# Gathered expert features: high and low parts in one tile, interleaved word by word

## The chip, the cores and the metric

The kernel runs on one core of a Trainium2 chip. The metric is device time in microseconds (us) from start to end of one execution; the figure given is the median of several.

## What is computed

Two layers of a streaming encoder for 256 prompt tokens and 64 running tokens (320 in all, D_MODEL 1024), float32. Each layer mixes three head groups and then applies a feed-forward part; in the second layer this is a mixture of eight SwiGLU experts of width 3584, of which each token uses two:

```python
logits = jnp.dot(xt, w_r, preferred_element_type=F32)
top_v, top_i = lax.top_k(logits, TOP_K)
w = jax.nn.softmax(top_v, axis=-1)
gates = jnp.einsum('tk,tke->te', w, jax.nn.one_hot(top_i, N_EXPERTS, dtype=F32))
...
for e in range(N_EXPERTS):
    h = jax.nn.silu(xt @ wg[e]) * (xt @ wu[e])
    y = y + gates[:, e:e + 1] * jnp.dot(h, wd[e], preferred_element_type=F32)
```

## The kernel before

Every large product is made with numbers split in two: a high part in float32r (TensorE's reduced float32) and a low part that is what the rounding left. A product is three matmuls: high by high, low by high, high by low.

The dense part (layers 1 and 2 without the experts) takes weights in cuts of 1024 words a partition as the stationary operand and the 320 tokens as the moving one (`three`, L1986 and following; the helper's line is L1981).

The experts run after it, one after another. For each, up to 128 tokens are gathered by row into `xg`, transposed by TensorE in eight blocks of 128 (`xg_T`, L2419; the helper's line is L1984) into two PSUM banks, and split there: ACT scales and rounds each block to `xgT_hi` (`xg_hi`, L1249), DVE computes what is left into `xgT_lo` (`xg_lo`, L1817). Both are tiles of 128 partitions, 8 blocks (`KB`), 128 tokens. They are the stationary operands of gate and up; the expert's weights move, 512 columns at a time.

Weights come in pieces of 2048 words a partition (1 MB), 42 pieces (`NP`) an expert: 14 of gate and 14 of up, taken in turns, then 14 of down. SyncE issues one DMA a piece into `raw`, seven slots deep, each as soon as DVE has released the slot. ACT rounds the piece to `split_hi` (L1207), DVE computes `split_lo` (L1808), both three slots deep (`SR`). TensorE (`experts`, L2439) makes twelve matmuls of a piece: for gate and up, high weights by `xgT_hi` (L2475) and by `xgT_lo` (L2479), then low weights by `xgT_hi` (L2484); in the very first piece the ones by `xgT_lo` come last (L2489). After silu and product (`hm`), four transposes (L2528) turn each 512 columns of hidden values; they load `hm[:, m % 2, k:512:4]`, every fourth word, as their stationary operand, and ACT and DVE split the result into `hmT_hi` and `hmT_lo`, the stationary operands of down (L2510, L2513, L2519, and L2495, L2496, L2502 for the last piece).

At `X_AT`, the third piece from the end of an expert (`NP - 3`), ACT and DVE make the next expert's `xgT_hi` and `xgT_lo` between their pieces; TensorE transposes `xg` four pieces earlier. The order on every engine is the program's; the waits are semaphores.

The last expert's output isn't scattered by DMA but placed by matmuls (L2544 to L2552). Its high and low parts are `last_y_hi` and `last_y_lo`, which before lie in the memory of `xgT_hi` and `xgT_lo`, and are the moving operand there.

Of the kernel before, what the change touches and what calls it, by code (L numbers as in the profile page):

```python
# [17 lines left out]
FR = mybir.dt.float32r  # L18
# [7 lines left out]
P = 128  # L26
D = 1024
KB = D // P
# [220 lines left out]
def build(nc, A, O):  # L249
# [5 lines left out]
    with ExitStack() as ctx:  # L255
        def sb(name, shape, dt=F32, stack=ctx):
            return stack.enter_context(nc.sbuf_tensor(name, shape, dt))
# [197 lines left out]
        isc_s = sb("isc_s", [P, 1], U32)  # L455
        last_token = sb("last_token", [P, 48])[:, 0:1]
        xg = sb("xg", [P, D])
        xgT_hi = sb("xgT_hi", [P, KB, P], FR)
        xgT_lo = sb("xgT_lo", [P, KB, P], FR)
        hs = sb("hs", [P, 2, 512])  # L460
        first_only = ExitStack()
        Gown = sb("Gown", [P, NT, P], F32, first_only)
# [3 lines left out]
        loop_only = ExitStack()  # L466
        hmT_lo = sb("hmT_lo", [P, FEB, P], FR, loop_only)
        loop_only.close()

        def raw_piece(i):  # L470
            s = PSLOT[i % PR]
            return raw[:, s * PIECE:(s + 1) * PIECE]
# [90 lines left out]
            eng.wait_ge(cv_out, 16 * 2 * DEPTH)  # L563

        HALVES = [slice(0, 512), slice(512, 1024)]
        last_y_hi = xgT_hi[:].rearrange("p k n -> p (k n)")
        last_y_lo = xgT_lo[:].rearrange("p k n -> p (k n)")

        def y_rows_of(t, c):
            return y_p[0, P * t:P * t + P, c] if t < 2 else y_s[0, :, c]  # L570
# [2036 lines left out]
```

## Time and profile before

| | |
|---|---|
| time, median of 3 runs | 1535.76 us (1535.21 to 1536.22) |
| span of the profiled execution | 1535.8 us |
| PE busy | 1527.8 us (99%), 8428 matmuls |
| PEld busy (weight loads) | 1333.0 us (87%) |
| DVE busy | 1234.4 us (80%) |
| ACT busy | 998.9 us (65%) |
| POOL busy | 217.5 us (14%) |
| DMA | 437.43 MB, mean 285 GB/s |

The span goes from the first to the last instruction of the profiled execution, which has no time of its own beside it. PE is TensorE's matmuls, PEld its weight loads, which overlap them; matmuls are pipelined, and the recorded length of one reaches into the next, so the distance between starts is what paces the engine. L12 is line 12 of the kernel.

### The profile page before, as it was taken

The page shows a single profiled execution, that of the slowest core. Times are in us where ns is not written, and L with a number is a line of the kernel's source. Part 1 is how long each engine was busy: PE and PEld are TensorE (multiplying, and loading weights), DVE is VectorE, ACT ScalarE, POOL GpSimd, SP SyncE. Part 2 cuts the span into 40 slices and gives each one's busy share as a digit, 9 for nine tenths or more (in the row PEclk, how much of TensorE's full clock was granted, in tenths as well). Part 3 has the DMA queues.
Part 4 walks back from the last instruction along what each step waited for, and adds up shares of the span by engine and source line. Part 5 has one row for each costly group of instructions (what it writes and reads, how often), then busy time and mean ns, then how long its engine had stood idle before and what let it go on. Part 6 is the DMA issues. An engine that isn't in the chain of part 4 may idle for free.

```text
span 1535.8 us, 21611 instructions
## 1 busy us (share of the span) xinstructions
PE 1527.8 (99%) x8428; PEld 1333.0 (87%) x8428; DVE 1234.4 (80%) x1253; ACT 998.9 (65%) x1079; POOL 217.5 (14%) x249
## 2 busy tenths in 40 slices
PE   9999999999999999999999999999999999999998
PEld 7989999999998988888888888888888888888887
DVE  5877666654477758988988888998998988898897
ACT  5655433333466547777777778777777777777775
POOL 5514400001150403101001001002002002002000
PEclk9999999999999999999999999999999999999999
DMA  8333455444443459999999999999999999999994
GB/s 226 96 110 116 149 164 164 133 157 151 125 122 110 141 209 367 383 366 388 372 381 376 374 374 376 391 359 386 384 363 382 381 362 379 400 361 363 394 373 183
DMA packets 159701, 437.43 MB, mean 285 GB/s; under 512 B 12068, under 2 KB 66176, under 8 KB 145264
## 3 DMA queue, kind: packets, MB, share of 16 engines
q1 hardware_dynamic: 151796, 423.02, 75.0%
q0 software_dynamic: 5552, 9.62, 2.3%
q10 hardware_dynamic: 2252, 3.41, 0.7%
q8 instruction: 68, 1.11, 0.3%
q14 instruction: 33, 0.27, 0.1%
HBM read 429.40 MB, written 13.60 MB: 288 GB/s over the span
## 4 chain that ended last, share of the span: by engine, by line
PE 98%; DMA 0%; ACT 0%; DVE 0%; issue 0%; SPq 0%; DVEq 0%; ACTq 0%
PE bank L1981 34%; PE bank L2475 13%; PE bank L2484 13%; PE bank L2479 13%; PE bank L2510 6%; PE bank L2513 6%; PE bank L2519 6%; PE bank L1984 3%; PE bank L2528 2%; PE bank L2496 0%; PE bank L2502 0%; PE bank L2495 0%; DMA gla<-b_g 0%; DVE x L1972 0%; ACT L1076 0%
## 5 line engine op out<-in xcount | busy, mean ns | idle before, releaser
L1808 DVE TENSOR_TENSOR split_lo<-raw,split_hi 128x2048 fp32r<-128x2048 f32 x336 | 763.1, 2289 | 101.8 <-ACT split_hi L1207 100.8
L1207 ACT CAST split_hi<-raw 128x2048 fp32r<-128x2048 f32 x336 | 640.5, 1911 | 224.5 <-PE bank L2484 145.7
L2475 PE MATMUL bank<-split_hi,xgT_hi 128*128 128x512 f32 x896 | 291.7, 395 | 0.0
L2479 PE MATMUL bank<-split_hi,xgT_lo 128*128 128x512 f32 x892 | 285.8, 390 | 0.0
L2484 PE MATMUL bank<-split_lo,xgT_hi 128*128 128x512 f32 x896 | 239.9, 390 | 0.0
L913 ACT CAST cut_hi<-ring 128x1024 fp32r<-128x1024 f32 x124 | 129.9, 1048 | 166.6 <-PE bank L1981 166.6
L1981 PE MATMUL bank<-xT_hi,cut_hi 128*128 128x320 f32 x752 | 236.7, 315 | 0.0
L1981 PE MATMUL bank<-xT_hi,cut_lo 128*128 128x320 f32 x752 | 233.5, 310 | 0.0
L1981 PE MATMUL bank<-xT_lo,cut_hi 128*128 128x320 f32 x752 | 231.9, 308 | 0.0
L1346 DVE TENSOR_TENSOR cut_lo<-ring,cut_hi 128x1024 fp32r<-128x1024 f32 x124 | 153.0, 1235 | 80.7 <-ACT cut_hi L913 79.9
L2484 PEld LDWEIGHTS bank<-split_lo,xgT_hi 128*128 128x128 f32 x896 | 168.3, 188 | 34.9
L2479 PEld LDWEIGHTS bank<-split_hi,xgT_lo 128*128 128x128 f32 x892 | 167.7, 188 | 34.7
L2475 PEld LDWEIGHTS bank<-split_hi,xgT_hi 128*128 128x128 f32 x896 | 166.2, 189 | 32.3
L1981 PEld LDWEIGHTS bank<-xT_hi,cut_hi 128*128 128x128 f32 x752 | 142.1, 189 | 1.6
L1981 PEld LDWEIGHTS bank<-xT_lo,cut_hi 128*128 128x128 f32 x752 | 142.2, 189 | 0.0
L1981 PEld LDWEIGHTS bank<-xT_hi,cut_lo 128*128 128x128 f32 x752 | 142.0, 189 | 0.0
L2510 PE MATMUL bank<-split_hi,hmT_hi 128*128 128x512 f32 x416 | 129.8, 393 | 0.0
L2513 PE MATMUL bank<-split_hi,hmT_lo 128*128 128x512 f32 x416 | 128.3, 390 | 0.0
L2519 PE MATMUL bank<-split_lo,hmT_hi 128*128 128x512 f32 x416 | 111.3, 390 | 0.0
L853 POOL COPY idc<-idx 128x1 uint32 (+1 forms) x8 | 5.7, 707 | 635.9 <-PE bank L1984 616.0
L2513 PEld LDWEIGHTS bank<-split_hi,hmT_lo 128*128 128x128 f32 x416 | 78.2, 188 | 16.3
L2519 PEld LDWEIGHTS bank<-split_lo,hmT_hi 128*128 128x128 f32 x416 | 78.1, 188 | 16.2
(316 smaller groups left out, 1723.2 us busy)
## 6 DMA issues: line engine op xcount, KB each, us to landing
raw<-moe_w_gate SPq DMA_DIRECT2D x112, 1024.0 KB, 7.8
raw<-moe_w_up SPq DMA_DIRECT2D x112, 1024.0 KB, 7.6
raw<-moe_w_down SPq DMA_DIRECT2D x112, 1024.0 KB, 7.3
ring<-w_in SPq DMA_DIRECT2D x15, 1024.0 KB, 5.5
ring<-ffn_w_gate SPq DMA_DIRECT2D x11, 1024.0 KB, 5.5
ring<-ffn_w_up SPq DMA_DIRECT2D x11, 1024.0 KB, 5.4
ring<-ffn_w_down SPq DMA_DIRECT2D x10, 1024.0 KB, 5.1
ring<-w_out SPq DMA_DIRECT2D x8, 1024.0 KB, 5.0
```

Source lines behind the costliest of these rows:

```text
L913: nc.scalar.copy(split_cut(cut_hi, q), raw_cut(q)).then_inc(cut_hi_ready, 1)
L1207: return nc.scalar.copy(split_hi[:, i % SR, :], raw_piece(i)).then_inc(hi_ready, 1)
L1346: V.tensor_tensor(split_cut(cut_lo, q), raw_cut(q), split_cut(cut_hi, q).bitcast(F32), ALU.subtract).then_inc(cut_lo_ready, 1)
L1808: V.tensor_tensor(split_lo[:, i % SR, :], raw_piece(i), split_hi[:, i % SR, :].bitcast(F32), ALU.subtract).then_inc(lo_ready, 1)
L1981: return TE.matmul(out, lhsT, rhs, start=start, stop=stop)
L1984: return TE.transpose(out, in_, ident[0:rows, 0:rows])
L2475: TE.matmul(o, xgT_hi[:, kk, :], hi[:, w * k + 512 * c:w * k + 512 * c + 512], start=kk == 0, stop=False)
L2479: TE.matmul(o, xgT_lo[:, kk, :], hi[:, w * k + 512 * c:w * k + 512 * c + 512], start=False, stop=False)
L2484: last = TE.matmul(o, xgT_hi[:, kk, :], lo[:, w * k + 512 * c:w * k + 512 * c + 512], start=False, stop=kk == KB - 1)
L2510: TE.matmul(banks[6 + n][:], hmT_hi[:, b, :], hi[:, c], start=b == 0, stop=False)
L2513: TE.matmul(banks[6 + n][:], hmT_lo[:, b, :], hi[:, c], start=False, stop=False)
L2519: last = TE.matmul(banks[6 + n][:], hmT_hi[:, b, :], lo[:, c], start=False, stop=b == FEB - 1)
```

## The change

The two tiles become one with a last dimension of two: word 0 is the high part, word 1 the low part of the same token. `xgT_hi` and `xgT_lo` are views of it. So ACT's and DVE's writes, DVE's read of the high part, and the stationary operands at L2475, L2479, L2484 and L2489 step by two words. `last_y_hi` and `last_y_lo` get tiles of their own, placed on the stack over the memory of `hmT_lo`.

```diff
--- before.py
+++ after.py
@@ -455,8 +455,8 @@
         isc_s = sb("isc_s", [P, 1], U32)
         last_token = sb("last_token", [P, 48])[:, 0:1]
         xg = sb("xg", [P, D])
-        xgT_hi = sb("xgT_hi", [P, KB, P], FR)
-        xgT_lo = sb("xgT_lo", [P, KB, P], FR)
+        xgT = sb("xgT", [P, KB, P, 2], FR)
+        xgT_hi, xgT_lo = xgT[:, :, :, 0], xgT[:, :, :, 1]
         hs = sb("hs", [P, 2, 512])
         first_only = ExitStack()
         Gown = sb("Gown", [P, NT, P], F32, first_only)
@@ -466,6 +466,8 @@
         loop_only = ExitStack()
         hmT_lo = sb("hmT_lo", [P, FEB, P], FR, loop_only)
         loop_only.close()
+        last_y_hi = sb("last_y_hi", [P, D], FR)
+        last_y_lo = sb("last_y_lo", [P, D], FR)
 
         def raw_piece(i):
             s = PSLOT[i % PR]
@@ -563,8 +565,6 @@
             eng.wait_ge(cv_out, 16 * 2 * DEPTH)
 
         HALVES = [slice(0, 512), slice(512, 1024)]
-        last_y_hi = xgT_hi[:].rearrange("p k n -> p (k n)")
-        last_y_lo = xgT_lo[:].rearrange("p k n -> p (k n)")
 
         def y_rows_of(t, c):
             return y_p[0, P * t:P * t + P, c] if t < 2 else y_s[0, :, c]
```

## Rows read from the trace of the kernel before

**Rows 1.** The page: the span, and TensorE's granted clock in tenths, 40 slices.
```profile
span 1535.8 us, 21611 instructions
...
PEclk9999999999999999999999999999999999999999
```

**Rows 2.** Busy us (x instructions) of PE, PEld, DVE, ACT, POOL; clock, DMA share, GB/s.
```profile
0.00:560.00 560.00, 557.00 (x3986) 528.24 (x3987) 371.78 (x654) 267.80 (x522) 133.28 (x172) 0.99 0.45 140
...
576.50:1527.00 950.50, 950.47 (x4325) 791.73 (x4325) 845.25 (x549) 719.45 (x541) 81.75 (x74) 1.00 0.98 371
```

**Rows 3.** The chain of work that ended last, shares of the span by line.
```profile
PE bank L1981 34%; PE bank L2475 13%; PE bank L2484 13%; PE bank L2479 13%; PE bank L2510 6%; PE bank L2513 6%; PE bank L2519 6%; PE bank L1984 3%; PE bank L2528 2%; PE bank L2496 0%; PE bank L2502 0%; PE bank L2495 0%; DMA gla<-b_g 0%; DVE x L1972 0%; ACT L1076 0%
```

**Rows 4.** Groups by line and form: count, busy us, mean ns, idle before.
```profile
L2475 PE MATMUL bank<-split_hi,xgT_hi 128*128 128x512 f32 x896 | 291.7, 395 | 0.0
L2479 PE MATMUL bank<-split_hi,xgT_lo 128*128 128x512 f32 x892 | 285.8, 390 | 0.0
L2484 PE MATMUL bank<-split_lo,xgT_hi 128*128 128x512 f32 x896 | 239.9, 390 | 0.0
...
L2475 PEld LDWEIGHTS bank<-split_hi,xgT_hi 128*128 128x128 f32 x896 | 166.2, 189 | 32.3
...
L2528 PEld LDWEIGHTS bank<-const_sb,hm 128*128 128x128 f32 x224 | 35.6, 204 | 4.5 <-DVE hm L1946 0.5
...
L1984 PEld LDWEIGHTS bank<-const_sb,xg 128*128 128x128 f32 x64 | 7.5, 140 | 1.0
```

**Rows 5.** Timeline of one gate piece: start us, us, engine, line, operation.
```profile
766.56 0.39 PE L2475 MATMUL bank<-split_hi,xgT_hi 128*128 128x512 f32 x1
766.56 0.19 PEld L2479 LDWEIGHTS bank<-split_hi,xgT_lo 128*128 128x128 f32 x1
...
768.37 0.39 PE L2484 MATMUL bank<-split_lo,xgT_hi 128*128 128x512 f32 x1
```

**Rows 6.** Timeline around the transposes of hm (L2528).
```profile
771.87 0.85 PE L2484 MATMUL bank<-split_lo,xgT_hi 128*128 128x512 f32 x3
...
772.56 0.63 PE L2528 MATMUL bank<-const_sb,hm 128*128 128x128 f32 x4
...
773.26 0.39 PE L2479 MATMUL bank<-split_hi,xgT_lo 128*128 128x512 f32 x1
```

**Rows 7.** Timeline around the transposes of xg (L1984).
```profile
678.63 0.85 PE L2519 MATMUL bank<-split_lo,hmT_hi 128*128 128x512 f32 x3
...
679.32 1.03 PE L1984 MATMUL bank<-const_sb,xg 128*128 128x128 f32 x8
...
680.66 0.62 PE L2513 MATMUL bank<-split_hi,hmT_lo 128*128 128x512 f32 x2
```

**Rows 8.** Timeline in the dense part, matmuls of 320 columns.
```profile
300.24 0.31 PE L1981 MATMUL bank<-xT_hi,cut_lo 128*128 128x320 f32 x1
300.24 0.19 PEld L1981 LDWEIGHTS bank<-xT_hi,cut_hi 128*128 128x128 f32 x1
...
301.41 0.31 PE L1981 MATMUL bank<-xT_lo,cut_hi 128*128 128x320 f32 x1
```

**Rows 9.** Timeline before the change from the first to the second expert.
```profile
684.99 2.16 ACT L1255 ACTIVATE xgT_hi<-bank,pcol 128x128 fp32r<-128x128 f32 x8
...
687.33 2.15 DVE L1823 SCALAR_TENSOR_TENSOR xgT_lo<-bank,pcol,xgT_hi 128x128 fp32r<-128x128 f32 x8
...
689.40 6.69 DVE L1808 TENSOR_TENSOR split_lo<-raw,split_hi 128x2048 fp32r<-128x2048 f32 x3
...
694.71 0.62 PE L2502 MATMUL bank<-split_lo,hmT_hi 128*128 128x512 f32 x2
```

**Rows 10.** Timeline at the start of the experts.
```profile
575.33 1.12 DVE L1823 SCALAR_TENSOR_TENSOR xgT_lo<-bank,pcol,xgT_hi 128x128 fp32r<-128x128 f32 x4
...
578.42 1.08 PE L2489 MATMUL bank<-split_hi,xgT_lo 128*128 128x512 f32 x4
```

**Rows 11.** Timeline at the last y, ACT's first write of it.
```profile
1526.55 0.69 ACT L1315 ACTIVATE xgT_hi<-bank,now_w 128x512 fp32r<-128x512 f32 x1 [4.66 <-PE bank L2502]
```

## The prediction

> **What bounds the kernel now.** I read the page first. TensorE is granted full speed nearly throughout (one slice of tenths after another is 9) over a span of 1535.8 us [rows 1]. The busy time by stretches then shows two parts: the two layers' dense work up to about 560 us, and the experts from 576.5 to 1527 us, where PE is busy 950.47 of 950.50 us at a clock of 1.00 (2.4 GHz), while DVE has 845 us, ACT 719 us, and the DMA engines are at 0.98 of their time [rows 2]. The chain of waits puts 13% of the span on each of L2475, L2479 and L2484 [rows 3]: these are the matmuls whose stationary operand the change touches.
>
> A busy PE is not yet a paced PE, so I went to the timeline of one piece. From the L2475 at 766.56 to the first L2484 at 768.37 there are eight matmuls: 1.81 us / 8 = 226 ns each [rows 5]. 512 columns at 2.4 GHz are 213.3 ns, so 13 ns come on top. There is no gap at the seam of a piece. The load of the next weights starts in the same hundredth of a microsecond as the matmul before it (766.56 and 766.56) and takes 0.19 us, so it ends some 38 ns before its own matmul starts [rows 5]. The experts' stretch is therefore set by a chain of matmuls 226 ns apart; loads run beneath it.
>
> How many are touched: 896 at L2475, 892 at L2479 and 896 at L2484 [rows 4], and 4 at L2489 (the first piece, where L2479 is skipped), 2688 in all. One ns on each is 2.7 us. I take 0.2% of the median, 3.1 us, as what can be told from no change, so 1.14 ns per matmul is the border.
>
> **The change, part by part.** No instruction is added or removed; operand patterns change, and a pair of tiles takes another place.
>
> *Stationary reads with a step of two words (2688 loads).* The trace has no load with this step, but one on either side. The transposes of hm at L2528 load `hm[:, m % 2, k:512:4]`, a step of four words; those of xg at L1984 a step of one. Mean load 204 against 140 ns [rows 4]. A load's record is longer than what it costs, so I take the spacing. Four transposes with step four: from 772.56 to the L2479 at 773.26 are 0.70 us, less the one L2475 between (0.226) leaves 0.474, or 118 ns each [rows 6]. Eight with step one: 679.32 to the L2513 at 680.66 are 1.34 us, less two L2510 (0.453), or 111 ns each [rows 7]. There the loads pace the engine, since 128 columns need only 53 ns. So a step of four costs about 7 ns where nothing covers it. A step of two I put between 0 and 7 ns, at 0 to 4. Here it is covered: a load at 111 to 118 ns lies under a matmul of 226. Cost 0. If the cover were gone, 7 ns x 2688 = 18.8 us.
>
> The cover also holds in the dense part: loads of the same kind, 0.19 us long, run under matmuls of 320 columns that start 146 ns apart (300.24 to 301.41, eight of them) [rows 8]. So even a recorded load longer than the spacing does not hold the matmuls up.
>
> The Trainium skill's SBUF page (SBUF — State Buffer, "Door 1: The DMA port swizzle", the note on cachelines) says that SBUF is read in lines of 16 bytes, that two hits in a line absorb the access, and that each further line costs. By that rule a step of two fp32 words (two hits) adds nothing to a load and a step of four (one hit) does. By it the sum would be 0 even with no cover; by interpolating my two rows it would be up to 4 ns a load uncovered, and 0 covered. The 118 against 111 ns agrees with its second half; no run yet shows the first.
>
> *The matmul that runs above such a load.* Could the extra reads slow the moving operand? The last L2484 of a piece runs while the first step-four load is under way: three L2484 take from 771.87 to 772.56, 0.69 us [rows 6]. The last L2519 before the xg transposes runs above a step-one load: three take from 678.63 to 679.32, also 0.69 us [rows 7]. No difference within 0.01 us. I take 0; one hundredth is 10 ns on one matmul, 27 us over 2688, so these rows alone leave that much open.
>
> *Writes and reads with step two on ACT and DVE.* L1255 (ACT) writes xgT_hi, L1823 (DVE) reads it and writes xgT_lo, eight instructions each at every change of expert. ACT takes 2.16 us from 684.99, DVE 2.15 us from 687.33, then three split_lo of 2.23 us each end at 691.63, 693.86 and 696.09 [rows 9]. The tightest need is the second one's, by L2502 at 694.71: 694.71 - 693.86 = 0.85 us of slack. So 0.85 us on eight instructions (106 ns each, on some 270) is free. I know no row with such a step; bounds are no change and a doubling. I take no change, since each instruction handles only 128 elements a partition, so most of its 270 ns is not elements. Behind ACT stand the casts of the next pieces, behind DVE the release of raw, thus SP's next DMAs; seven boundaries matter (the eighth expert's prefetch feeds nothing). At the start of the experts the first L1823 group ends at 576.45, and L2489 uses it at 578.42: 1.97 us of cover [rows 10]. Cost 0.
>
> *The last y.* last_y_hi and last_y_lo leave the xgT tiles for space over hmT_lo. They stay contiguous, are the moving operand at L2544 to L2550, and their waits are the same (the write at 1526.55 waits for left_done) [rows 11]. The blocks of hmT_lo still being read then are the last two; no wait is added. Cost 0.
>
> **Sum.** 0 + 0 + 0 + 0. The profiled execution's span is 1535.8 us and the median of the timed runs 1535.76, so nothing is to be added for what lies around the span: 1535.8 us, own range 1534.3 to 1537.3, from noise (the three runs lie within 1 us) and half a ns a matmul either way.
>
> **Rivals.**
> - *The load steals from the moving read* (slower, 0.10). The time beyond the columns is 13.3 ns at 512 columns and 146 - 133.3 = 12.7 ns at 320 [rows 5, 8]: a constant, about 32 cycles, and a unit-step load of 128 words covers 32 runs of four words. If each such run took a cycle from the moving stream, step two makes 64 of them: +13.3 ns x 2688 = +35.8 us, 1571.6 us. Against it: at step four it would be 128, and the L2484 above it should take 53 - 13 = 40 ns more; three take 0.69 us in both places [rows 6, 7]. But those loads belong to transposes, whose records are shorter at step one (140 against 188 ns) [rows 4], so the comparison isn't the same kind of load. It decides from 1.14 ns a matmul.
> - *Loads lose their cover* (slower, 0.04). If the load's record grew as at L2528, 204/140 x 188 = 274 ns, and counted in full, each matmul would take 47 ns more: +126 us, 1662 us. Against: dense matmuls 146 ns apart with 188 ns loads [rows 8], and a spacing that grew by only 7 ns. It needs an uncovered load of over 226 ns, twice the 111. The skill's tensor page (TensorE: Matmul & The Clock Gate, "The mechanism") also says that a load overlaps matmuls in flight only where the row group differs. By that rule the up to 4 ns would come out in full, 10.8 us, 1546.5 us; but rows 5 show a full-height load entirely beneath a full-height matmul, so the trace disagrees.
> - *The boundary's ACT and DVE work becomes late* (slower, 0.06). Doubled, DVE's eight add 2.15 us, of which 1.30 stand beyond the 0.85 us of slack: x7 = 9.1 us, 1544.9 us. It decides from 1.3 us a boundary in all, 0.44 us beyond the slack. For it: the slack is small. Against: the instruction's fixed part.
> - *Faster* (0.08). High and low parts now share lines, and reads of one could ease the other. At 2 ns a matmul 5.4 us, 1530.4 us; at most the whole 13.3 ns, 35.8 us. No row shows the 13 ns moving with the stationary operand.
>
> **How the numbers follow.** Unchanged has 0.72; the three slower rivals 0.20 together; faster 0.08. The range starts in the faster case at 1 ns a matmul (1533.0) and reaches to 1541, which takes in 2 ns a matmul slower and the smaller half of the boundary rival; the 1571.6 and 1662 cases and the rest of the tails (about 2 in 10) are left out.
>
> **What would show it.** Loads at L2475, L2479 and L2484 at 188 to 200 ns; the eight matmuls of a piece still 1.81 us; three matmuls before L2528 still 0.69; L1255 and L1823 at 0.38 and 0.34 us mean; span 1535.8. The prediction is wrong if the spacing of these three lines moves off 226 ns while L2510, L2513 and L2519 stay (a matter of the operand), or if PE idles at the first L2502 of an expert (the boundary).

## The result, and the profile after

The changed kernel takes 1552.76 us (median of 4 runs, 1551.55 to 1554.29), the kernel before 1535.61 us on the same chip (1535.21 to 1536.22, 4 runs): ratio 1.0107, interval 1.0094 to 1.012. It is slower by about 17 us, where 1535.8 us was forecast and the range ended at 1541. The profiled execution has a span of 1552.1 us against 1535.8 in [rows 1].

The busy time by stretches of the kernel after, with the columns of [rows 2] (the experts' stretch is closed 16 us later, since the first write of the last y, at 1526.55 in [rows 11], now comes at 1542.85, 16.3 us later):

```profile
0.00:560.00 560.00, 557.13 (x3987) 528.45 (x3988) 372.02 (x655) 267.90 (x522) 133.21 (x172) 0.99 0.45 140
...
576.50:1543.00 966.50, 966.50 (x4322) 806.21 (x4322) 845.29 (x549) 718.69 (x541) 81.95 (x73) 1.00 0.98 364
```

The dense part is as before. The 16.3 us by which the last y comes later are the whole growth of the span, so all of it lies before that write and behind the dense part. PE is busy without a gap in both stretches, the granted clock is 1.00 in both, and DVE and ACT do the same work in the same time (845.29 and 718.69 us against 845.25 and 719.45). PE gained no idle time and no instruction: its matmuls take longer. The groups by line and form tell which, with the columns of [rows 4] (L1255 and L1823 are the writers of the tile):

```profile
L2475 PE MATMUL bank<-split_hi,xgT 128*128 128x512 f32 x896 | 296.0, 399 | 0.0
L2479 PE MATMUL bank<-split_hi,xgT 128*128 128x512 f32 x892 | 290.3, 394 | 0.0
L2484 PE MATMUL bank<-split_lo,xgT 128*128 128x512 f32 x896 | 245.5, 395 | 0.0
...
L2475 PEld LDWEIGHTS bank<-split_hi,xgT 128*128 128x128 f32 x896 | 171.5, 194 | 32.4
...
L2528 PEld LDWEIGHTS bank<-const_sb,hm 128*128 128x128 f32 x224 | 35.7, 204 | 4.2
...
L1255 ACT ACTIVATE xgT<-bank,pcol 128x128 fp32r<-128x128 f32 x72 | 19.7, 388 | 0.4 <-PE bank L1981 0.4
L1823 DVE SCALAR_TENSOR_TENSOR xgT<-bank,pcol,xgT 128x128 fp32r<-128x128 f32 x72 | 19.5, 343 | 1.5 <-ACT xgT L1255 1.5
```

A recorded load grew from 189 to 194 ns, a recorded matmul by 4 or 5 ns. The record of a pipelined matmul is modelled, so the distance between starts decides. One gate piece on the timeline, TensorE's matmuls alone, beside [rows 5]:

```profile
767.73 0.39 PE L2475 MATMUL bank<-split_hi,xgT 128*128 128x512 f32 x1
...
769.59 1.09 PE L2484 MATMUL bank<-split_lo,xgT 128*128 128x512 f32 x4
...
772.39 1.10 PE L2484 MATMUL bank<-split_lo,xgT 128*128 128x512 f32 x4
773.33 0.63 PE L2528 MATMUL bank<-const_sb,hm 128*128 128x128 f32 x4
```

Eight matmuls take 1.86 us, 233 ns each, where [rows 5] have 1.81 us, 226. Over all start-to-start distances of gate and up in the two traces (2576 each, gaps at other work left out) the means are 227.2 and 233.4 ns; those of down (L2510, L2513, L2519) are 226.9 and 227.1. With those gaps taken in, the time from each start at L2475, L2479 or L2484 to the next matmul's start adds up to 614.8 us before and 631.2 after: 16.5 us, 6.1 ns a matmul, the whole difference. Below, "spacing" is the mean without the gaps, worked out from the starts in each trace. The spacing of down, which hardly any run touches, lies between 226.9 and 227.2 in all of them, so 0.3 ns is what can be read.

The change of expert, where the forecast put its slower rival, is not late. The first to the second expert, beside [rows 9]:

```profile
687.09 2.18 ACT L1255 ACTIVATE xgT<-bank,pcol 128x128 fp32r<-128x128 f32 x8
...
689.43 2.15 DVE L1823 SCALAR_TENSOR_TENSOR xgT<-bank,pcol,xgT 128x128 fp32r<-128x128 f32 x8
691.50 6.68 DVE L1808 TENSOR_TENSOR split_lo<-raw,split_hi 128x2048 fp32r<-128x2048 f32 x3
...
696.82 0.62 PE L2502 MATMUL bank<-split_lo,hmT_hi 128*128 128x512 f32 x2
```

DVE's eight instructions still take 2.15 us, and the matmul that needs split_lo follows on the one before it without a wait.

### The profile page after: what moved, and what is told of

It reads as the page before. It is cut to its first block, busy times and chain, and to the rows that moved or that the text cites. A ratio compares the mean times of both kernels' runs of the same rounds, so it can differ in the third digit from the quotient of the medians.

```text
span 1552.1 us, 21611 instructions
## 1 busy us (share of the span) xinstructions
PE 1544.2 (99%) x8428; PEld 1347.9 (87%) x8428; DVE 1234.5 (80%) x1253; ACT 998.5 (64%) x1079; POOL 217.7 (14%) x249
## 4 chain that ended last, share of the span: by engine, by line
PE 98%; DMA 0%; ACT 0%; DVE 0%; issue 0%; SPq 0%; DVEq 0%; ACTq 0%
PE bank L1981 34%; PE bank L2475 14%; PE bank L2484 13%; PE bank L2479 13%; PE bank L2513 6%; PE bank L2510 6%; PE bank L2519 6%; PE bank L1984 3%; PE bank L2528 2%; PE bank L2502 0%; PE bank L2495 0%; PE bank L2496 0%; DMA gla<-b_g 0%; DVE x L1972 0%; ACT L1076 0%
## 5 line engine op out<-in xcount | busy, mean ns | idle before, releaser
L2475 PE MATMUL bank<-split_hi,xgT 128*128 128x512 f32 x896 | 296.0, 399 | 0.0
L2479 PE MATMUL bank<-split_hi,xgT 128*128 128x512 f32 x892 | 290.3, 394 | 0.0
L2484 PE MATMUL bank<-split_lo,xgT 128*128 128x512 f32 x896 | 245.5, 395 | 0.0
L2484 PEld LDWEIGHTS bank<-split_lo,xgT 128*128 128x128 f32 x896 | 173.3, 193 | 36.1
L2479 PEld LDWEIGHTS bank<-split_hi,xgT 128*128 128x128 f32 x892 | 172.7, 194 | 34.8
L2475 PEld LDWEIGHTS bank<-split_hi,xgT 128*128 128x128 f32 x896 | 171.5, 194 | 32.4
L2510 PE MATMUL bank<-split_hi,hmT_hi 128*128 128x512 f32 x416 | 129.6, 393 | 0.0
L2513 PE MATMUL bank<-split_hi,hmT_lo 128*128 128x512 f32 x416 | 128.3, 390 | 0.0
L2519 PE MATMUL bank<-split_lo,hmT_hi 128*128 128x512 f32 x416 | 111.4, 389 | 0.0
L2513 PEld LDWEIGHTS bank<-split_hi,hmT_lo 128*128 128x128 f32 x416 | 78.1, 188 | 16.4
L2519 PEld LDWEIGHTS bank<-split_lo,hmT_hi 128*128 128x128 f32 x416 | 78.1, 188 | 16.4
```

What stands on the lines that cost most here:

```text
L2475: TE.matmul(o, xgT_hi[:, kk, :], hi[:, w * k + 512 * c:w * k + 512 * c + 512], start=kk == 0, stop=False)
L2479: TE.matmul(o, xgT_lo[:, kk, :], hi[:, w * k + 512 * c:w * k + 512 * c + 512], start=False, stop=False)
L2484: last = TE.matmul(o, xgT_hi[:, kk, :], lo[:, w * k + 512 * c:w * k + 512 * c + 512], start=False, stop=kk == KB - 1)
L2510: TE.matmul(banks[6 + n][:], hmT_hi[:, b, :], hi[:, c], start=b == 0, stop=False)
L2513: TE.matmul(banks[6 + n][:], hmT_lo[:, b, :], hi[:, c], start=False, stop=False)
L2519: last = TE.matmul(banks[6 + n][:], hmT_hi[:, b, :], lo[:, c], start=False, stop=b == FEB - 1)
```

## The experiments

### Is it the step? Four layouts

**blocks**: the changed kernel, but high and low part of a block lie one after the other; one tile, last_y moved, every step one.

```diff
-        xgT = sb("xgT", [P, KB, P, 2], FR)
-        xgT_hi, xgT_lo = xgT[:, :, :, 0], xgT[:, :, :, 1]
+        xgT = sb("xgT", [P, KB, 2, P], FR)
+        xgT_hi, xgT_lo = xgT[:, :, 0, :], xgT[:, :, 1, :]
```

> High and low parts share one tile as in the change, but as neighbouring blocks of 128 words, so every stationary operand has a step of one again; last_y keeps its own tiles. Theory A (the step of two is the whole cost): matmuls of gate and up 227 ns apart as in the kernel before, time 1535.6 us, within 1 us. Rival B (the sharing of one tile or the new place of last_y costs): 233 ns apart and about 1552 us.

Measured: ratio 0.9998 (0.9989 to 1.0008), spacing 227.2 ns, loads 188. The shared tile and the moved last_y cost nothing that shows.

**step2_k, step4_k, step8_k**: the kernel before with its two tiles kept apart; in each, 2, 4 or 8 blocks of the same part are interleaved, so that the step is 2, 4 or 8 words. Readers and writers are indexed likewise.

```diff
-        xgT_hi = sb("xgT_hi", [P, KB, P], FR)
-        xgT_lo = sb("xgT_lo", [P, KB, P], FR)
+        xg_hi_t = sb("xgT_hi", [P, KB // 2, P, 2], FR)
+        xg_lo_t = sb("xgT_lo", [P, KB // 2, P, 2], FR)
...
-                                TE.matmul(o, xgT_hi[:, kk, :], hi[:, w * k + 512 * c:w * k + 512 * c + 512], start=kk == 0, stop=False)
+                                TE.matmul(o, xg_hi_t[:, kk // 2, :, kk % 2], hi[:, w * k + 512 * c:w * k + 512 * c + 512], start=kk == 0, stop=False)
```

> Two separate tiles as before, but in each the blocks k and k+1 are interleaved word by word: a step of two without mixing high and low parts. Theory A (step alone): 233 ns apart, 1552 to 1553 us. Rival C (mixing high and low words in one line is what costs): 227 ns, 1535.6 us.

> Two separate tiles, four blocks interleaved: a step of four words, so each word of a stationary operand lies in another run of four words. Theory L (the cost grows with the number of such runs a load touches, 32, 64, 128 for steps one, two, four): 6.5 ns for 32 more runs, so about 20 ns for 96 more, 246 ns apart, 2688 x 20 = 53 us, about 1589 us. Rival P (the read fetches pairs of words, so a step of two is already the worst): 233 ns, about 1553 us. Rival D (cost grows with the step itself, 6.5 ns for each word of it beyond one): also 246 ns here, so the step of eight tells it from L.

> Two separate tiles, all eight blocks interleaved: a step of eight words. Theory L (runs of four words touched): as the step of four, 246 ns and about 1589 us. Rival P: 233 ns and about 1553 us. Rival D (cost by the step itself): 7 x 6.5 = 45 ns, 272 ns apart, about 1658 us.

| kernel | time, us | ratio (interval) | load record, ns | spacing, ns |
|---|---|---|---|---|
| blocks, step 1 | 1536.97 | 0.9998 (0.9989-1.0008) | 188 | 227.2 |
| step2_k | 1551.77 | 1.0091 (1.0074-1.0108) | 193 | 233.3 |
| step4_k | 1564.00 | 1.0174 (1.0157-1.0191) | 311 | 235.4 |
| step8_k | 1592.21 | 1.0351 (1.0333-1.0368) | 329 | 245.1 |

The kernel before on this chip: 1537.36 (single executions go from 1535.35 at a granted clock of 1.000 to 1539.68 at 0.996). step2_k shows the change's cost without mixing the two parts: the same spacing, and 14.4 us, with an interval that overlaps the change's. With blocks, which has the shared tile at no cost, that leaves the step of the stationary operand alone as the cause. One piece of step2_k, then loads and writers of step4_k by form, then a wait of step4_k (us in total, times, longest):

```profile
764.76 0.63 PE L2475 MATMUL bank<-split_hi,xgT_hi 128*128 128x512 f32 x2
...
766.62 1.09 PE L2484 MATMUL bank<-split_lo,xgT_hi 128*128 128x512 f32 x4
```

```profile
L2475 PEld LDWEIGHTS bank<-split_hi,xgT_hi 128*128 128x128 f32 x896 | 249.4, 311 | 0.4
...
L1823 DVE SCALAR_TENSOR_TENSOR xgT_lo<-bank,pcol,xgT_hi 128x128 fp32r<-128x128 f32 x72 | 26.7, 453 | 1.3 <-ACT xgT_hi L1255 1.3
L1255 ACT ACTIVATE xgT_hi<-bank,pcol 128x128 fp32r<-128x128 f32 x72 | 20.9, 493 | 0.4 <-PE bank L1981 0.4
```

```profile
PEld bank L2502 <- DVE split_lo L1808: 2.1, 8, 0.3
```

The extra spacing is 0, 6, 8 and 18 ns at steps 1, 2, 4 and 8. None of the stated laws gives that row: it neither doubles with the step nor stands still from step four on. The load record makes one jump between two and four. At step four the boundary rival also shows: DVE's instruction takes 110 ns more, eight are 0.88 us where 0.85 were free, and L2502 waits for split_lo. Steps four and eight lose something at the transposes too: from the last matmul before four L2528 (L2484 in 48 of the 56 places, L2519 in 8) to the second one after them is 0.94 us before and 1.05 us at either step (medians). The sums close: step4_k 8.2 ns x 2688 + 0.09 us (means) x 56 = 27 us, measured 26.6; step8_k 17.9 x 2688 + 0.10 x 56 = 53.7, measured 54.9.

### Is it a price for each stepped load, or for each word loaded?

**hi_step2**: step2_k with the high part alone stepped; the low tile as before.

```diff
+        xg_hi_t = sb("xgT_hi", [P, KB // 2, P, 2], FR)
+        xg_lo_t = sb("xgT_lo", [P, KB // 1, P, 1], FR)
```

> Only the high tile has a step of two (blocks k and k+1 interleaved), the low one keeps step one, all else as before: 1792 of the 2688 loads step by two. Theory S (each stepped load costs its own matmul's spacing a fixed 6.5 ns, whatever the others do): 1792 x 6.5 = 11.6 us, about 1547.5 us; spacings where both loads at hand are stepped 233, where neither is 227. Rival M (the low part's loads or the mere mixture set the pace): 1535.6 or 1552 us.

Measured: 1550.38 us against 1537.59, ratio 1.0081 (1.0064 to 1.0098), spacing 232.0 ns. A third of the loads is unstepped, yet the cost is 12.8 us, where step2_k's is 14.4. The time alone doesn't reject a fixed price for each stepped load, whose forecast was 11.6 us: the interval is 2.6 us wide to either side. The spacings do: where a low part's matmul follows another, with an unstepped load beneath, they stand 231 ns apart (382 distances), not 227. So a load of step one, among stepped ones, also runs off 227.

**half_unit** (the kernel before) and **half_step2** (the kernel after): gate and up load only the first 64 of the 128 stationary columns; tokens 64 to 127 of a group are not computed.

```diff
-                        outs = [banks[2 * up + (FC * h + m) % 2][:] for m in ms]
+                        outs = [banks[2 * up + (FC * h + m) % 2][0:64] for m in ms]
...
-                                TE.matmul(o, xgT_hi[:, kk, :], hi[:, w * k + 512 * c:w * k + 512 * c + 512], start=kk == 0, stop=False)
+                                TE.matmul(o, xgT_hi[:, kk, 0:64], hi[:, w * k + 512 * c:w * k + 512 * c + 512], start=kk == 0, stop=False)
```

> The kernel before, with gate and up computed for the first 64 gathered tokens alone: each of the 2688 stationary operands has 64 columns in place of 128 at step one, the moving operand keeps its 512 columns; the other 64 rows hold what was there. Theory T (a load takes a share of the moving stream's time for each word it reads): the 13.3 ns beyond the 512 columns fall to about 6.7, 220 ns apart, 2688 x 6.7 = 18 us less, about 1518 us. Rival F (13.3 ns is a fixed price of changing the stationary operand): 227 ns apart and 1535.6 us.

> The changed kernel with the same halving, 64 stationary columns at a step of two. Theory T: half of what the step costs with 128 columns, so about 3.3 ns above the halved kernel with step one. Rival F (a fixed price of a stepped operand): 233 ns apart, 6.5 ns above the halved kernel with step one.

Measured: 1.0038 (1.0024 to 1.0052) and 1.0045 (1.0028 to 1.0062). half_unit by form and on the timeline:

```profile
L2475 PEld LDWEIGHTS bank<-split_hi,xgT_hi 128*64 128x64 f32 x896 | 120.1, 135 | 76.8
```

```profile
764.77 0.40 PE L2475 MATMUL bank<-split_hi,xgT_hi 128*64 128x512 f32 x1
...
766.62 1.08 PE L2484 MATMUL bank<-split_lo,xgT_hi 128*64 128x512 f32 x4
```

The load is 135 ns instead of 188 and the matmuls stand further apart: 1.85 us for eight, spacing 229.9 at either step. Half the load costs some 6 us, and at half the width step two costs nothing beyond it: neither 3.3 nor 6.5 ns, as the two theories had it. If a load took time from the moving read word by word, half of it would have given time back. That theory falls, and with it the forecast's first rival. The Trainium skill (TensorE: Matmul & The Clock Gate, "Step-by-step: what each phase is for") says that TensorE reads its two operands over two ports, so that a load takes no read bandwidth from a running matmul. The half load agrees with it; that the spacing moves with the load all the same, by up to 6.7 ns here, is a thing that sentence doesn't cover.

**dense_step**: experts as before; the dense part's cuts are read word-interleaved, which makes their stationary step 8 (2 in the cuts of w_out and ffn_w_down).

```diff
-            return part[:, q % CR, :].rearrange("p (k n) -> p k n", k=2 if CUTS[q][2] in ("wo", "d") else KB)
+            return part[:, q % CR, :].rearrange("p (n k) -> p k n", k=2 if CUTS[q][2] in ("wo", "d") else KB)
```

> Experts as before; in the dense part the split weights, the stationary operand there, are laid out with the block number innermost: a step of two words in the cuts of w_out and ffn_w_down, a step of eight in all others, under matmuls of 320 columns, which stand 147 ns apart before. If the step of two costs per load and not per moving column, those with step two stand 153 ns apart. For the step of eight, theory R (a load's own time, its record less some 75 ns, so 254 ns, paces the engine where the matmul is shorter): about 250 ns apart, some 100 ns x 2784 = 290 us more, about 1825 us. Rival C (a step of eight costs a fixed 18 ns a matmul, as it did under 512 columns): 165 ns apart, about 1590 us.

Measured: 1759.14 us, ratio 1.1445 (1.1422 to 1.1467). Loads by form (step 8, then step 2), and a stretch of step 8:

```profile
L1981 PEld LDWEIGHTS bank<-xT_hi,cut_lo 128*128 128x128 f32 x752 | 255.4, 340 | 0.0
...
L1981 PEld LDWEIGHTS bank<-hT_hi,cut_hi 128*128 128x128 f32 x176 | 34.2, 194 | 0.0
```

```profile
299.61 0.41 PE L1981 MATMUL bank<-xT_lo,cut_hi 128*128 128x320 f32 x1
...
300.17 0.34 PEld L1981 LDWEIGHTS bank<-xT_lo,cut_hi 128*128 128x128 f32 x1
...
300.41 0.34 PEld L1981 LDWEIGHTS bank<-xT_hi,cut_lo 128*128 128x128 f32 x1
...
301.54 0.40 PE L1981 MATMUL bank<-xT_hi,cut_hi 128*128 128x320 f32 x1
```

At step 8 the matmuls of 320 columns stand 1.93 us / 8 = 241 ns apart (146 before; 243 in the mean of 2149 distances), nearly the 245 of 512 columns in step8_k. The spacing hardly depends on the moving columns any more: there the loads pace TensorE, one every 0.24 us, each record reaching into the next. Theory R had the spacing nearly right (250) and the time 66 us too long, in the main because it counted 2784 matmuls: 528 of those have step two, and 2256 x 96 ns = 217 us of the 222 measured. At step 2 they stand 147 ns apart (eight in 1.18 us from 520.05), as before. So step 8 is a lost cover and step 2 isn't, and under 320 columns step 2 is free.

### Where does step two cost? Maps over widths

**map_unit** and **map_step2** (before and after): in gate and up, stationary columns M by group of pieces and moving columns N by expert; what is beyond is not computed, so only the spacing counts. The same edit in both:

```diff
+                        M = (128, 112, 64, 128)[min(q // 8, WIDE)]
+                        N = (512, 480, 448, 384, 320, 256)[h] if count > 2 else 512
...
+                                TE.matmul(o, xgT_hi[:, kk, 0:M], hi[:, w * k + 512 * c:w * k + 512 * c + N], start=kk == 0, stop=False)
```

> A map with step one. The kernel before, but in the first six experts the gate and up matmuls move 512, 480, 448, 384, 320 and 256 columns (one value an expert), and their stationary operands have 128, 112, 64 and 128 columns in the four groups of chunks; the left out columns and rows are not computed. The time is of no use, the spacing of starts inside a piece is. Theory F (fixed price at step one): columns / 2.4 GHz + 13.3 ns everywhere where that is above the 112 ns of a load. Rival Q (the price depends on how the load's length falls against the matmul's): the 64-column operand, 230 ns with 512 columns, differs from the 128-column one by other amounts with other numbers of columns.

> The same map with the changed kernel's step of two. Theory F: 6.7 ns above the map with step one, whatever the number of moving columns. Rival Q: 6.7 ns at 512 columns, none at 320 (the dense part showed none there), with a border between; with 112 stationary columns (a load as short as the 128-column one with step one) either no price at 512 columns, if the load's length is what counts, or the same 6.7 ns, if the step itself does.

Spacing less N / 2.4 (the time of N columns at the granted 2.4 GHz), in ns; distances more than some 40 ns above that are left out. From 384 columns down they are many, since TensorE then waits for weights and its granted clock falls to one half for 3 to 7 us at a time, so those rows say less.

| N | step 1: M = 128, 112, 64 | step 2: M = 128, 112, 64 |
|---|---|---|
| 512 | 13.7, 16.7, 16.6 | 20.2, 13.9, 17.0 |
| 480 | 16.6, 19.5, 17.0 | 18.9, 13.4, 17.8 |
| 448 | 16.9, 13.6, 15.7 | 16.7, 17.3, 15.0 |
| 384 | 15.2, 13.6, 13.7 | 13.8, 15.4, 13.7 |
| 320 | 12.8, 13.4, 12.6 | 13.5, 13.5, 12.4 |
| 256 | 12.8, 10.0, 8.2 | 13.4, 13.3, 11.1 |

Theory F falls twice: the price at step one isn't 13.3 ns everywhere (at N = 512 and 480 it goes from 13.7 to 19.5), and the step doesn't add the same to it. Step two costs 6.5 ns at 128 by 512, and at 112 by 512 and 112 by 480 the stepped operand is the faster one, by 2.8 and 6.1 ns.

**fine_unit** and **fine_step2**: N stays 512, eighteen widths M (`M = (128, 126, 124, ... 96, 80)[3 * h + q // 8]`).

> Step one, 512 moving columns, stationary operands of 128, 126, 124, 122, 120, 118, 116, 114, 112, 110, 108, 106, 104, 102, 100, 98, 96 and 80 columns in the first three groups of gate and up of the first six experts (left out tokens are not computed); only the spacing is of use. Theory Q (the load's length against the matmul's sets the spacing): it goes up and down between 227 and 233 ns as the load shortens, in bands of several columns. Rival N (any operand of fewer than 128 columns costs 3 ns, whatever its length): 230 ns from 126 columns down.

> The same 18 lengths at a step of two. Theory Q: the same ups and downs as at step one, shifted by the columns whose load time the step adds (5 to 6 ns, or 6 to 7 columns at 0.85 ns each, and fewer for shorter operands): 233 ns at 128, falling to 227 ns at or before 120 columns, where the load is as long as the full one at step one. Rival S (the step itself is paid at full width): 233 ns down to some width with no relation to the load's record.

| M | 128 | 126 | 124 | 122 | 120 | 118 | 116 | 114 | 112 |
|---|---|---|---|---|---|---|---|---|---|
| step 1 | 227.5 | 233.3 | 228.3 | 231.1 | 233.2 | 231.9 | 233.3 | 230.3 | 229.1 |
| step 2 | 233.3 | 231.1 | 233.3 | 230.0 | 233.0 | 230.1 | 233.3 | 231.8 | 227.3 |

| M | 110 | 108 | 106 | 104 | 102 | 100 | 98 | 96 | 80 |
|---|---|---|---|---|---|---|---|---|---|
| step 1 | 233.3 | 230.0 | 230.0 | 228.9 | 230.9 | 233.3 | 228.9 | 230.1 | 233.3 |
| step 2 | 226.7 | 232.5 | 233.3 | 228.9 | 231.1 | 230.0 | 233.2 | 230.7 | 230.7 |

Spacing in ns, 91 to 95 distances each (128: nearly 1000). At either step it moves up and down between 226.7 and 233.3 ns, 13.3 to 20 above the columns' own time. At step one the loads get shorter all the way, from 188 ns (M = 128) to 148 (M = 80), while the spacing doesn't follow; and a record of 187 or 188 ns goes with 227.5 ns at step one (128) and with 233.0 at step two (120). So the length of the load's record alone doesn't decide. 126 columns of step one cost as much as the change. Rival N, 230 ns from 126 columns down, doesn't hold either.

**m112_unit** and **m112_step2** take the one width where the map has step two at the bottom, now timed: before and after with `0:112` in place of `0:64` above. Tokens 112 to 127 of a group are not computed.

> The kernel before with stationary operands of 112 columns in all of gate and up (the last 16 gathered tokens are not computed). Theory Q, from the 230 ns in the map: 2688 x 3.2 = 8.6 us more than the kernel before, about 1544 us, though each load is shorter. Rival (less loaded, never slower): 1535.6 us or less.

> The changed kernel with stationary operands of 112 columns at a step of two. Theory Q, from the 227 ns in the map: the whole cost of the change is gone, about 1536 us. Rival (the step itself costs): about 1552 us, or 6.5 ns x 2688 above the 112-column kernel with step one, 1561 us.

Measured: m112_unit 1.0031 (1.002 to 1.0042), spacing 229.0; m112_step2 1.0000 (0.9991 to 1.001), spacing 226.9. One piece of m112_step2, and its loads:

```profile
764.12 0.39 PE L2475 MATMUL bank<-split_hi,xgT 128*112 128x512 f32 x1
...
765.93 1.07 PE L2484 MATMUL bank<-split_lo,xgT 128*112 128x512 f32 x4
```

```profile
L2475 PEld LDWEIGHTS bank<-split_hi,xgT 128*112 128x112 f32 x896 | 157.9, 179 | 39.6
```

With the layout of the change and 112 columns the whole cost is gone: 1.81 us for eight. The kernel before with 112 columns is slower: (229.0 - 227.2) x 2688 = 4.8 us, and 0.31% is 4.8 us. The ups and downs of the map repeat to about 1 ns: 230.0, 229.1 and 229.0 in three kernels at step one, 227.2, 227.3 and 226.9 at step two.

### The one step-four load that the kernel before has

L2528 loads every fourth word of hm. **hm_unit** lets DVE write hm in the other order (neighbouring results 128 words apart), so that the load has step one; **down_rows** takes the rows of the down weights in another order, so that DVE's write stays as it is too. The edit of down_rows:

```diff
-            wd_v = A["moe_w_down"][0].rearrange("e (c p b) n -> e c p b n", b=4, p=P)
+            wd_v = A["moe_w_down"][0].rearrange("e (c b p) n -> e c p b n", b=4, p=P)
...
-                            last = TE.transpose(tb[n % 2][:, 128 * k:128 * k + 128], hm[:, m % 2, k:512:4], ident)
+                            last = TE.transpose(tb[n % 2][:, 128 * k:128 * k + 128], hm[:, m % 2, 128 * k:128 * k + 128], ident)
```

> The kernel before with hm written by DVE in the transposes' order (writes 128 words apart), so that the 224 loads of L2528 have a step of one in place of four; xgT stays as before. If uncovered stepped loads cost the 7 to 10 ns a load that the spacing of the transposes showed, 224 x 9 = 2.0 us less: about 1533.6 us, ratio 0.9987. If DVE's stepped writes are slow (over 0.8 us more for each L1946) the next split_lo is late and it is slower than before.

> The kernel before with the rows of the down weights given to the partitions as c, b, p in place of c, p, b, so that the transposes of hm load 128 neighbouring words (step one) and DVE writes hm as before; each DMA of a down piece then reads runs of 4 KB in place of 8 KB, as those of gate and up do. The 224 transposes stand 109 ns apart as in the kernel with the reordered hm, the loads' records fall from 204 to 140 ns, DVE's L1946 stays at 744 ns: some 9 ns x 224 = 2.0 us less, about 0.13%, ratio 0.9987. If the down pieces' DMAs become late, PE waits at L2510 and it is slower than before. It is the only version of this study that could be faster than both.

hm_unit: ratio 1.0053 (1.0041 to 1.0065), slower; by form:

```profile
L1946 DVE SCALAR_TENSOR_TENSOR hm<-bank,now_w,hs 128x512 f32<-128x512 f32 x56 | 59.9, 1139 | 0.0
...
L2529 PEld LDWEIGHTS bank<-const_sb,hm 128*128 128x128 f32 x224 | 26.0, 140 | 15.1 <-DVE hm L1946 8.2 <-issue 2.6
```

The loads fell to 140 ns, but DVE's instruction rose from 744 to 1139 ns, and TensorE waits for it: 8.2 of the 15.1 us before the loads of L2529, where the kernel before had 0.5 of 4.5. down_rows has the short loads (140 ns) and L1946 at 744; its ratio is 0.9998 (0.9989 to 1.0007). Its transposes stand 109 ns apart instead of 117 (means of 168 distances), 224 x 8 ns = 1.8 us in all, which the timed runs don't resolve. No version beat the kernel before by what can be told.

## Why the prediction was wrong

**The reading of what bounds the kernel was right.** All of the 16 us was added in the experts' chain of matmuls, with PE busy throughout, and the forecast had named its own alarm: the three lines moved off 226 ns, L2510, L2513 and L2519 stayed.

**The step that failed is "Stationary reads with a step of two words": "Here it is covered ... Cost 0", with its twin "The matmul that runs above such a load": "I take 0".** The load is indeed covered: its record (194 ns) ends some 40 ns before its own matmul, as at 189. Being covered didn't make it free. The time beyond the columns' own, which the forecast read as a constant of 13 ns, moves between 13.3 and 20 ns at 512 columns with the load that runs beneath, and the change took it from the bottom to the top: 6.1 ns on each of 2688 matmuls, 16.5 us. Three readings led there:

- 13.3 ns at 512 columns and 12.7 at 320 agreed by chance: at 480 or 448 columns, or with 126 stationary ones, the kernel before would have shown 17 or 20. "No row shows the 13 ns moving with the stationary operand" holds for its rows, but the trace of before does show the 13 ns moving, in the matmuls that follow a break. From the L2479 at 773.26 in [rows 6] to the line below are seven distances, 1.61 us, 230 ns each:

```profile
774.87 1.07 PE L2484 MATMUL bank<-split_lo,xgT_hi 128*128 128x512 f32 x4
```

- The comparison above a transpose's load (0.69 us for three in both places) was of another kind of load, as the text itself said. And 0.69 us for three is 230 ns each, not 226: over the whole trace of before the last matmul above a transpose's load stands 232 to 233.5 ns from it, whether that load has step four (L2528) or one (L1984). So both rows already held a matmul that costs more than 226, for a reason that no run shows, and their likeness hid it. The ±10 ns that the text left open were kept out of the range.
- The dense rows (188 ns loads, 146 ns apart) were evidence against a lost cover, and rightly: dense_step shows step two free there. They said nothing of 512 columns.

One smaller step of the sum fails too: "nothing is to be added for what lies around the span". In every profiled run with a time of its own the time is 1.8 us above the span (1553.92 against 1552.1 for the changed kernel). It shifts both kernels alike (the timed runs of the kernel before show the same 1.8) and explains nothing of the 17 us.

**The size of the rivals.** "The load steals from the moving read" has the right sign and place, at 0.10, but not the mechanism, and its 35.8 us are twice what came: half the load costs more time, not less, and at 112 columns the stepped load is the faster one. "Loads lose their cover" is what steps of eight do, not of two. There the forecast's doubt about the record was right: it is 329 to 340 ns, what it costs is 241 to 245. The Trainium skill's rule that a load overlaps matmuls in flight only where the row group differs (TensorE: Matmul & The Clock Gate, "The mechanism") would have made even step two come out in full; the traces disagree, since even at step eight loads run beneath full-height matmuls, and beneath each other. The Trainium skill's rule of lines of 16 bytes (SBUF — State Buffer, "Door 1: The DMA port swizzle") fits the load records as far as step four, 188, 193 and then 311 ns at steps 1, 2 and 4, but not the 329 ns at step 8, which touches no more lines than step 4; the time of the kernel wasn't in it.

**The boundary** (0.06): right in kind, and right about the slack of 0.85 us, which step four used up (0.88). At step two DVE's instruction didn't change (343 ns) and ACT's rose by 9 ns, which nothing waits for. The argument for no change, that most of its 270 ns is not elements, is weak on the forecast's own rows: split_lo takes 2.23 us for 2048 elements, which makes an estimate of 140 ns for 128. So it was right about step two for a reason that isn't shown. **last_y** and the shared tile: cost 0, as blocks shows. **Faster**: no sign of it at 128 columns.

**What stays open.** Why the spacing takes the value it takes. It repeats from kernel to kernel, and it depends on stationary width, step and moving width together. The single distances in the traces do show a rhythm. In the kernel before, every distance of 229 ns or more in gate and up lies among the first ten after a break (transposes, or down's matmuls): the first eight have a mean of 229.8 ns (gaps left out), all later ones 226.7. In the kernel after these are 232.8 and 233.6, so what the step costs is the value into which the stream settles. At 112 columns of step one the settled stream repeats some 226, 229 and 231 ns in turn; at 64 columns it repeats six values from 225 to 236. What sets this pattern no run tells, and neither of the two simple laws tried (one value wherever the load isn't the original one; a curve that the step merely shifts) held. That step four's 235 ns lies outside the band because its loads nearly pace TensorE is argued from step eight, not shown.

## What to carry to other kernels

Where TensorE is the bound, "hidden under the matmul" doesn't make a weight load free: take start-to-start distances, some right after a break and eight in the middle of a stretch, before and after any change of a stationary operand's layout, width or step, because 6 ns on each of 2688 matmuls is 1% while both busy shares stay at 99%. Keep full-width stationary operands at step one unless a measurement says otherwise: here two cost 3% of a 512-column matmul and nothing of a 320-column one, and four and eight made the load's record 65 to 80% longer. A shorter load isn't always a faster stream (135 ns instead of 188 made it 0.4% slower here): measure the width, don't assume it.

## What the hardware showed that was not expected

- Fewer stationary columns made the stream slower: 64 columns +0.38%, 112 columns +0.31%, with loads of 135 and 174 ns instead of 188.
- At 112 columns a step of two is faster than a step of one (226.9 against 229.0 ns).
- ACT's write of 128 words a partition (L1255) takes 379, 388, 493 and 497 ns at steps 1, 2, 4 and 8. DVE's instruction beside it (L1823), which reads one operand and writes its result at that step, takes 343, 343, 453 and 456. DVE's 512 words of hm, written 128 words apart and read in order, take 1139 ns instead of 744 (hm_unit).
- After a break a stream of matmuls needs several of them to settle: 229.8 ns in the mean over the first eight distances of gate and up in the kernel before, 226.7 after that.
